# Contracting over 64 rows instead of 128 in the last of five matmuls of an attention score block

## The reference

```python
def mla_queries(p, q_norm_g, w_uq, rope):
    q = (rms_norm(p[..., O_CQ:O_CKV], q_norm_g) @ w_uq).reshape(b, t, 4, 128 + 64)
    q_nope, q_pe = q[..., :128], q[..., 128:]
    return concatenate([q_nope, apply_rope(q_pe, *rope)], axis=-1)

# k = [k_nope (4 heads x 128) | k_pe (64, one for all heads)], 1024 + 256 keys
s = jnp.einsum('bqhd,bkhd->bhqk', q, k) / math.sqrt(192)
o = jnp.einsum('bhqk,bkhd->bqhd', jax.nn.softmax(s), v)
```

## Time and profile before

| What | Value |
|---|---|
| median of 3 runs | 3349.19 us (3346.74 to 3349.64) |
| the profiled execution's own time | 3349.64 us |
| its span | 3347.8 us, granted TensorE clock 0.984 of full speed |
| PE busy | 3167.1 us (95%), 18680 instructions |
| DVE, ACT, POOL busy | 1455.5, 1054.1, 371.4 us |
| attention, first to last score matmul | 191.1 to 410.5 us |

### The profile page before, as it was taken

The page is one execution under the profiler, slowest core; times in us unless marked ns, Lnnn a source line. Parts: engine busy times, 40 slices in busy tenths (PEclk is TensorE's granted clock), DMA queues, the critical chain, the costliest instruction groups (busy, mean ns, idle before and its releaser), DMA issues.

```text
span 3347.8 us, 42668 instructions
## 1 busy us (share of the span) xinstructions
PE 3167.1 (95%) x18680; PEld 2442.8 (73%) x18680; DVE 1455.5 (43%) x2104; ACT 1054.1 (31%) x1616; POOL 371.4 (11%) x392
## 2 busy tenths in 40 slices
PE   6989999999899999999998989988889999999999
PEld 2468766666768888888876767766767788888787
DVE  6267725676444111113337353266653434344333
ACT  4244424434233111112224664334423322222111
POOL 1022202443212000000003000021112000000000
PEclk9999999999999999999999999989989999999999
DMA  6022210000041111112112101000022111111212
GB/s 245 32 71 71 74 54 13 13 26 13 1 170 69 51 51 40 49 44 88 48 49 93 60 26 38 6 6 3 2 102 82 45 51 51 51 38 38 101 40 74
DMA packets 35209, 182.33 MB, mean 54 GB/s; under 512 B 4261, under 2 KB 4261, under 8 KB 21584
## 3 DMA queue, kind: packets, MB, share of 16 engines
q1 hardware_dynamic: 22176, 133.18, 11.3%
q0 software_dynamic: 12848, 46.43, 3.6%
HBM read 161.63 MB, written 17.96 MB: 54 GB/s over the span
## 4 chain that ended last, share of the span: by engine, by line
PE 85%; DVE 8%; ACT 4%; DMA 1%; issue 1%; POOL 1%; DVEq 0%; POOLq 0%; ACTq 0%; SPq 0%
PE ps L547 18%; PE ps L548 18%; PE ps L549 18%; PE ps L537 9%; PE ps L686 4%; PE ps L750 3%; PE ps L591 2%; PE ps L1227 2%; DMA ar<-in_xT 1%; PE ps L833 1%; PE ps L608 1%; DVE ar L2088 1%; PE ps L1088 1%; PE ps L650 1%; ACT ar L1448 1%
## 5 line engine op out<-in xcount | busy, mean ns | idle before, releaser
L547 PE MATMUL ps<-r,r 128*128 128x512 f32 x2632 | 1047.6, 398 | 10.2 <-DVE r L2084 5.0
L549 PE MATMUL ps<-r,r 128*128 128x512 f32 x2632 | 1038.8, 395 | 0.0
L548 PE MATMUL ps<-r,r 128*128 128x512 f32 x2632 | 1038.7, 395 | 0.0
L547 PEld LDWEIGHTS ps<-r,r 128*128 128x128 f32 x2632 | 496.7, 189 | 136.4 <-issue 16.1
L548 PEld LDWEIGHTS ps<-r,r 128*128 128x128 f32 x2632 | 497.0, 189 | 116.4 <-issue 3.1
L549 PEld LDWEIGHTS ps<-r,r 128*128 128x128 f32 x2632 | 496.6, 189 | 115.2
L1410 ACT ACTIVATE r<-ar 128x1024 fp32r<-128x1024 f32 (+1 forms) x170 | 174.3, 1032 | 553.5 <-PE ps L549 511.5
L2077 DVE TENSOR_TENSOR r<-ar,r 128x1024 fp32r<-128x1024 f32 (+1 forms) x170 | 203.9, 1200 | 331.3 <-ACT r L1410 331.1
L1448 ACT ACTIVATE ar<-ps 128x256 f32<-128x256 f32 (+3 forms) x330 | 146.8, 470 | 501.4 <-PE ps L537 116.0
L537 PE MATMUL ps<-ar 128*128 128x128 f32 (+4 forms) x1460 | 246.6, 341 | 6.4 <-ACT ar L1448 3.3
L537 PEld LDWEIGHTS ps<-ar 128*128 128x128 f32 (+1 forms) x1460 | 191.9, 187 | 57.2 <-issue 31.8
(11 more groups left out here) (296 smaller groups left out, 3584.7 us busy)
## 6 DMA issues: line engine op xcount, KB each, us to landing
ar<-in_w_mod SPq DMA_DIRECT2D x24, 1024.0 KB, 5.0
ar<-in_w_gu SPq DMA_DIRECT2D x22, 1024.0 KB, 4.8
ar<-in_w_up SPq DMA_DIRECT2D x22, 1024.0 KB, 4.8
ar<-in_w_in SPq DMA_DIRECT2D x19, 1024.0 KB, 4.9
ar<-in_w_dn SPq DMA_DIRECT2D x32, 512.0 KB, 3.4
x<-ar POOLq DMA_DIRECT2D x48, 256.0 KB, 2.5
ar<-x POOLq DMA_DIRECT2D x24, 512.0 KB, 8.2
ar<-in_xT POOLq DMA_DIRECT2D x16, 512.0 KB, 13.3
```

The lines of the kernel that those rows point to most:

```text
L547: M.matmul(o, whk, hi[k][:, a:a + n], start=k == 0, stop=False)
L548: M.matmul(o, whk, lo_[k][:, a:a + n], start=False, stop=False)
L549: ins = M.matmul(o, wlk, hi[k][:, a:a + n], start=False, stop=k == nk - 1)
```

## The change

The fifth matmul of each column block reads rows 0 to 63 of both operands alone. With that nothing reads rows 64 to 127 of `low_pe`, and the two memsets that set them to zero are taken out, with POOL's wait on them.

```diff
@@ scores(u), TensorE
                     ins = dot(o[:, a:a + n], [(hi, keys), (hi, keys_lo), (low, keys), (both, kst[:, a:a + n]),
-                                              (low_pe, kst[:, a:a + n])])
+                                              (low_pe[0:64, :], kst[0:64, a:a + n])])
                 ins.then_inc(*product(("s", u)))
@@ GpSimd
             pool.wait_ge(*a_hi.at(("q", u)))
-            if u < 2:
-                G.memset(low_pe[64:128, :].bitcast(F32), 0.0).then_inc(*p_gate(("zeros", u)))
-                pool.wait_ge(*p_gate.at(("zeros", u)))
             G.tensor_tensor(low, qn[...], hi.bitcast(F32), ALU.subtract).then_inc(*p_gate(("ql", u)))
```

## The result

| | before | after |
|---|---|---|
| median of 4 runs each, us | 3349.41 (3346.74 to 3352.21) | 3388.20 (3383.55 to 3391.39) |
| ratio, with three more runs of the changed kernel counted in | | 1.0114, 95% interval 1.0100 to 1.0129 |
| span of the profiled execution, us | 3347.8 | 3383.5 |
| granted TensorE clock | 0.984 | 0.983 |

The changed kernel is slower, as forecast. The forecast of 3383.7 us is 4.5 us short of the median, which lies inside the range of 3372 to 3391 us.

A forecast was written before the change was run, and what follows sets the result against it. TensorE was taken to bound the kernel, with steady attention units hiding nothing. 33.4 us (units 3 to 31) + 1.0 (unit 0) - 0.3 (memset) = 34.1 on 3349.64 gave 3383.7 us, 1.0% slower, range 3372 to 3391.

The forecast's parts named there:

- The chain is TensorE's, and a steady unit hides nothing: Attention units of 7.08 us: TensorE has 85% of the waits; a nanosecond on the scores is one on the kernel.
- Half the rows save nothing: Fifth score matmuls: a pass takes its time for columns, so 64 rows in place of 128 save nothing.
- A change of shape costs 0.20 us, into transposes 0.15: Score matmuls: switching between 128 and 64 rows drains TensorE; five at 0.20 and one at 0.15 make 1.15 us a unit.
- The sum: Whole kernel: units 3 to 31 add 33.4 us, unit 0 adds 1.0, the memset gives 0.3 back: 34.1 us slower.
- The estimate from the Trainium skill: Price of a change of shape from matmul latency formulas: 0.163 us, which would make the forecast 3378.5 us.
- Units 1 and 2 hide their share: Attention start: growth of 1.35 us, and of 1.00 plus 0.15 draining, fits idle times of 1.56 and 1.23: nothing added.
- The memset is worth 0.3 us: Unit 0, POOL ahead of the first subtraction: without the memset it starts 0.29 us earlier, 0.3 us saved.
- Half the price: Rival, score blocks: array emptying or weight load is hidden, 0.10 us a change; 17.6 us slower, 3367 us; chance 0.05.
- no price: Rival, score blocks: a 64-row matmul doesn't count as a change of shape; 3349.3 us, no change; chance 0.04.
- Overlap: Rival, score blocks: the 64-row matmul runs beside its neighbour, saving 8.7 us with the memset; 3340.9 us; chance 0.02.
- The clock: Rival, attention: emptying TensorE halves its granted clock throughout, some 190 us more, about 3570 us; chance 0.01.
- the upper bound of 3391 us: Whole kernel: 0.21 us a change, units 1 and 2 not hiding theirs (2.3 us), 2 us lost to half clock: 41.6 us.

The follow-up runs named there:

- experiment 6: Fifth matmul left out in all three column blocks of the kernel before (measuring only): 3336.62 us, ratio 0.9963, unit 6.64 us.
- experiment 1: Changed kernel with a unit's three 64-row matmuls grouped at the end of its scores, two changes of shape: 3358.37 us, ratio 1.0028 to the kernel before.
- experiment 2: Changed kernel with the middle block's 64-row matmul put first in its block, four changes of shape: 3373.60 us, ratio 1.0070 to the kernel before.
- experiment 4: Kernel before with the fifth matmul cut to 64 rows, both memsets kept: 3387.99 us, ratio 1.0119, unit 8.23 us.
- experiment 8: Changed kernel with 32 rows in the fifth matmul, part of the product left out: 3390.36 us, ratio 1.0123 to the kernel before.
- experiment 7: Three 64-row matmuls grouped at a unit's end, the middle one reading rows 64 to 127, memsets kept: 3354.83 us, ratio 1.0015 to the kernel before.

## Why the prediction was right

- *The chain is TensorE's, and a steady unit hides nothing.* Right for a longer score block: the unit grew by 1.13 us and TensorE's idle time in it stayed at 0.39. The prediction said it of a shorter block too, and there it fails: in experiment 6 the softmax held up every second unit.
- *Half the rows save nothing.* Right. 96 rows take 402 ns, 32 rows make the same unit as 64, and the added time of a unit in experiments 1, 2, 4 and 8 and in the changed kernel is accounted for by changes of shape alone.
- *A change of shape costs 0.20 us, into transposes 0.15.* Right, and it was the term that decided. It was read from one place of the trace with other operands (fp32) and another stage, where 64-row passes stood between 128-row ones. For fp32r, which no row showed at 64 rows, it holds: 0.34, 0.75 and 1.13 us for two, four and six. The sum had 1.15 a unit, 0.02 too much, or 0.6 us in all. The rule of the Trainium skill (TensorEngine Tiling (Array Packing), Key Properties) that a change of the tiling mode drains the engine agrees with these runs, and so does its list under Available Configurations, which has rows of 32, 64 and 128 and none of 96: 96 rows cost nothing. The estimate from the Trainium skill, TensorE: Matmul & The Clock Gate, 0.163 us each, was too low. Of its two formulas, both for bf16, the second stands under Back-to-back issue gap, and neither has a term for a weight load. Whether the difference is that term was not tested.
- *Units 1 and 2 hide their share.* Right. Their idle time went from 1.56 and 1.23 us to 0.34 and 0.25, by 1.22 and 0.98, the 1.20 and 1.00 of their changes of shape. The 0.15 us that the prediction added each time for emptying does not show in it. The clock had no part: it was back at 1.00 by 196 us, in unit 0's scores.
- *The memset is worth 0.3 us.* Right: 0.26.
- *Half the price* and *no price* are excluded by the changed kernel's unit and by experiments 1, 2 and 4. *Overlap* is a true mechanism (experiment 7), but it needs a free half of the array, which neighbours of 128 rows leave none of, as the prediction argued. *The clock* stays at 1.00 in the steady units.
- *The remaining 4.5 us.* The sum was made for the profiled execution of before and gave 34.1 us; the spans differ by 35.7, the medians by 38.8. The prediction put the clock at nothing in its sum and at 2 us in its upper bound. In the profiled execution it cost 1.4 us, in unit 0. With the price 0.6 us too high, 1.0 us added behind the attention and ACT's rounding 0.25 us sooner, 34.1 - 0.6 + 1.4 + 1.0 - 0.25 = 35.65, the difference of the spans. In the medians the clock cost more. Runs of one kernel differ by their mean granted clock. Those at 0.984 were 3383.55 us for the changed kernel and 3384.46 for the matmul alone; the eight at 0.984 of the kernel before, beside the first four experiments, had a median of 3348.2. At equal clock the difference is 35 to 36 us. At 0.981 the changed kernel took 3391.39. So what was left out is some 3 us that the median run lost to half clock. That the upper bound of 3391 us held the median is in part luck: most of its room was for 0.21 us a change everywhere and for both covered units in the open, and neither came true. The mean clock of the 15 runs with six changes of shape is 0.982, that of the 37 runs of the kernel before beside the experiments 0.984, which points to more half clock with the change. Where in the kernel, and why, was not traced.

## What to carry to other kernels

Using fewer rows of the array did not make a matmul cheaper here, and a 64-row matmul between 128-row ones makes TensorE empty itself twice, here 0.2 us each time. Pad the contraction with zeros to 128 rows (or to 96, which is as good), or put matmuls of the small shape together, and in opposite halves; weigh the two changes that remain against what they save. Before a matmul is trimmed, look in the trace for a place where such shapes already meet: the ends of the matmuls and the gap in the weight loads give the price. Where a block is to get shorter, count the time to spare up to the weight load that waits next, not up to its matmul.

## What the runs showed of the hardware

- The price of a change of shape was 0.20 us in fp32 and in fp32r, and the same with 32 rows as with 64; between 96 and 128 rows it was nil.
- Two 64-row matmuls in opposite halves overlapped almost fully: three took 0.61 us where they took 0.85 in one half.
- The clock differs between executions in the first units. Behind 3 us without a matmul, 3.4 us at half clock came up in the changed kernel and in one with 128 rows throughout, a mean of 0.67 over 30 us with 32 rows, and none in the profile of the kernel before. The run to run spread of the changed kernel, 8 us, goes along with a mean clock of 0.981 to 0.984.
